# A two-layer hybrid decoder: the rope's exchange of partition blocks moved from a TensorE permutation matmul to on-chip transfers

## The reference, cut to what matters

```
def rope(x, positions):
    ...
    x1, x2 = xf[..., : d // 2], xf[..., d // 2:]
    return jnp.concatenate([x1 * cos - x2 * sin, x2 * cos + x1 * sin], axis=-1).astype(x.dtype)

def swa_branch(q, k, v, positions, sinks):
    ...
    q = rope(q.reshape(B, S, SWA_HEADS, SWA_HEAD_DIM), positions)
    k = rope(k.reshape(B, S, SWA_KV_HEADS, SWA_HEAD_DIM), positions)
```

## Time and profile before

| | |
|---|---|
| median of 3 runs | 1743.79 us (1743.47 to 1743.79) |
| the profiled execution | 1743.34 us |
| its span, first to last instruction | 1741.5 us |
| PE busy | 1713.2 us, 98% of the span |
| PEld, DVE, ACT, POOL busy | 1445.0, 1087.4, 853.1, 142.0 us |
| granted TensorE clock, mean | 0.998 of full |
| DMA engines, HBM read and written | 87 GB/s over the span |

### The profile page before, as it was taken

How to read it: one execution, slowest core, us unless ns; L and a number is a source line. 1 busy time by engine, 2 the same in 40 slices (tenths; PEclk the granted TensorE clock), 3 DMA queues, 4 the chain that set the end, 5 groups by cost and what they waited for, 6 DMA issues and landing times.

```text
span 1741.5 us, 21885 instructions
## 1 busy us (share of the span) xinstructions
PE 1713.2 (98%) x8634; PEld 1445.0 (83%) x8634; DVE 1087.4 (62%) x1494; ACT 853.1 (49%) x1203; POOL 142.0 (8%) x140
## 2 busy tenths in 40 slices
PE   8999999999999999999999999999999999999997
PEld 6888888888898888888888888888888988888886
DVE  7886886675557534354587777867654665343545
ACT  7576566665445414121466755666544453232223
POOL 0111211111200000000001111111111000000000
PEclk9999999999999999999999999999999999999999
DMA  4221122222342222222321211122224222232222
GB/s 155 67 69 61 61 71 64 73 73 85 114 141 73 97 97 97 97 97 97 110 91 64 76 61 61 61 73 73 72 84 156 77 97 97 97 97 97 97 97 73
DMA packets 47638, 152.36 MB, mean 87 GB/s; under 512 B 5296, under 2 KB 9776, under 8 KB 47536
## 3 DMA queue, kind: packets, MB, share of 16 engines
q1 hardware_dynamic: 45520, 147.02, 25.4%
q10 hardware_dynamic: 2016, 3.94, 0.6%
HBM read 146.75 MB, written 4.19 MB: 87 GB/s over the span
## 4 chain that ended last, share of the span: by engine, by line
PE 83%; issue 6%; DVE 5%; ACT 3%; POOL 1%; DMA 1%; SPq 0%; ACTq 0%; DVEq 0%; POOLq 0%
PE bank L557 77%; PE bank L562 3%; PE bank L815 1%; PE bank L866 1%; ACT w_hi L1018 1%; POOL mix L2271 1%; DMA x<-in_x 1%; DVE w_lo L1561 0%; DVE hf L1608 0%; PE bank L566 0%; PE bank L665 0%; DVE x L1617 0%; DVE fb L1807 0%; ACT dn L1075 0%; DVE h_lo L1596 0%
## 5 line engine op out<-in xcount | busy, mean ns | idle before, releaser
L557 PE MATMUL bank<-h_hi,w_hi 128*128 128x512 f32 (+1 forms) x1224 | 477.1, 390 | 7.0 <-DVE h_lo L1596 5.1
L557 PE MATMUL bank<-h_lo,w_hi 128*128 128x512 f32 (+1 forms) x1224 | 471.7, 385 | 0.0
L557 PE MATMUL bank<-h_hi,w_lo 128*128 128x512 f32 (+1 forms) x1224 | 471.6, 385 | 0.0
L1018 ACT ACTIVATE w_hi<-raw 128x1024 fp32r<-128x1024 f32 (+2 forms) x269 | 271.1, 1013 | 219.9 <-DMA raw<-in_w 219.4
L1561 DVE TENSOR_TENSOR w_lo<-raw,w_hi 128x1024 fp32r<-128x1024 f32 (+2 forms) x269 | 316.8, 1181 | 63.9 <-ACT w_hi L1018 57.4
L557 PEld LDWEIGHTS bank<-h_hi,w_hi 128*128 128x128 f32 x1224 | 230.0, 188 | 57.6 <-DVE h_lo L1596 7.3
L557 PEld LDWEIGHTS bank<-h_hi,w_lo 128*128 128x128 f32 x1224 | 229.9, 188 | 46.9
L557 PEld LDWEIGHTS bank<-h_lo,w_hi 128*128 128x128 f32 x1224 | 230.1, 188 | 44.7 <-issue 1.4
L557 PE MATMUL bank<-u_hi,w_hi 128*128 128x512 f32 (+1 forms) x560 | 208.0, 371 | 0.0
L557 PE MATMUL bank<-u_hi,w_lo 128*128 128x512 f32 (+1 forms) x560 | 207.7, 371 | 0.0
L557 PE MATMUL bank<-u_lo,w_hi 128*128 128x512 f32 (+1 forms) x560 | 207.7, 371 | 0.0
(11 more groups left out here) (261 smaller groups left out, 2744.4 us busy)
## 6 DMA issues: line engine op xcount, KB each, us to landing
raw<-in_w SPq DMA_DIRECT2D x251, 512.0 KB, 3.3
x<-in_x SPq DMA_DIRECT2D x16, 256.0 KB, 3.7
side_raw<-in_w SPq DMA_DIRECT2D x6, 512.0 KB, 4.9
x_spill<-x ACTq DMA_DIRECT2D x8, 256.0 KB, 2.2
x<-x_spill SPq DMA_DIRECT2D x8, 256.0 KB, 3.1
out_y<-x SPq DMA_DIRECT2D x8, 256.0 KB, 2.1
raw<-in_w SPq DMA_DIRECT2D x8, 192.0 KB, 2.4
raw<-in_w SPq DMA_DIRECT2D x8, 128.0 KB, 2.3
```

The costliest lines, as they stand in the source:

```text
L557: mm = pe.matmul(o, s, m, start=start and i == 0 and j == 0, stop=last and i == n - 1 and j == 2, skip_group_check=True)
L1018: act.activation(chunk_in(gc, w_hi, side_hi)[:, 0:w], chunk_in(gc, raw, side_raw)[:, 0:w], ACT.Copy)\
```

## The change: what it does

`rp_hi` becomes a float32 copy `rp` of the tile. After it ACT waits until that copy is complete, then (from the second rope tile on) until `rot_used` says that the previous exchanged tile has been read, and then issues four transfers of 32 partitions by 512 floats (64 KB) each, from `rp` to `rp_turned`, each block from its partner. All four count up one semaphore, `rot`, by 16 each. DVE no longer makes `rp_lo`, waits for all four transfers, and reads `rp_turned` in SBUF in place of `rot_bank` in PSUM. `rotate` and its five calls in a layer are gone from TensorE.

```
--- before.py
+++ after.py
@@ -284,8 +284,8 @@
         cf = place("cf", [P, 3, SEQ], F32, r1 + 16384)
         ra = place("ra", [P, SEQ], F32, r1 + 16384 + 6144)
         rb = place("rb", [P, SEQ], F32, r1 + 16384 + 8192)
-        rp_hi = place("rp_hi", [P, SEQ], F32R, r1 + 16384 + 10240)
-        rp_lo = place("rp_lo", [P, SEQ], F32R, r1 + 16384 + 12288)
+        rp = place("rp", [P, SEQ], F32, r1 + 16384 + 10240)
+        rp_turned = place("rp_turned", [P, SEQ], F32, r1 + 16384 + 12288)
         later_f = place("later_f", [P, 768], F32, r1 + 24576)
         later_hi = place("later_hi", [P, 640], F32R, r1 + 24576 + 3072)
         later_lo = place("later_lo", [P, 640], F32R, r1 + 24576 + 5632)
@@ -361,8 +361,7 @@
         mv_ones = signal("mla_v_ones", 2)
         trig_r = signal("trig_scaled", 2)
         rp_h = signal("rope_in_hi", 5)
-        rp_l = signal("rope_in_lo", 5)
-        rot = signal("rotated", 5)
+        rot = signal("rotated", 5 * 4 * 16)
         rot_used = signal("rot_used", 5)
         rp_sum = signal("rope_sum", 5)
         rpo_h = signal("rope_out_hi", 5)
@@ -765,14 +764,6 @@
                     own = slice(h % 2, h % 2 + 2)
                     values(h, CAUSAL, lambda j: (mv_hi[:, j, h // 2, own, :], mv_lo[:, j, h // 2, own, :]))
 
-                def rotate(n):
-                    pe.wait_ge(*rp_l(n + 1))
-                    if n:
-                        pe.wait_ge(*rot_used(n))
-                    pe.matmul(rot_bank[:, :], cst[:, SWAP, :], rp_hi[:, :], start=True, stop=False)
-                    pe.matmul(rot_bank[:, :], cst[:, SWAP, :], rp_lo[:, :], start=False, stop=True)\
-                      .then_inc(rot.sem, 1)
-
                 def band_scores(t):
 
                     pe.wait_ge(*rpo_l(t + 2))
@@ -922,13 +913,10 @@
                             tile(("swa_k",), h_hi, h_lo, None, between)
                         elif h == HEADS - 2:
                             tile(("swa_vt",), h_hi, h_lo, None, between)
-                            rotate(0)
 
                     turn(("swa_v",), ("swa_vt",), vt_at(None))
-                    rotate(1)
                     tile(("swa_q", 1), h_hi, h_lo)
                     band_scores(0)
-                    rotate(2)
                     tile(("swa_q", 2), h_hi, h_lo)
                     pe.wait_ge(*freed(("swa_v",)))
                     pe.wait_ge(*wv_ones(2))
@@ -941,8 +929,6 @@
                         band_shift(n)
                         out_tile(0, n + 1)
                         band_shift(n + 1)
-                        if t < 2:
-                            rotate(t + 3)
                         if t + 1 < PAIRS:
                             tile((("swa_q", 3), ("stick", 0, 0), ("stick", 0, 1))[t], h_hi, h_lo)
                         band_values(n)
@@ -1127,8 +1113,14 @@
                 def rope(n, name, scale):
                     tile_ready(name)
                     if n:
-                        act.wait_ge(*rot(n))
-                    act.activation(rp_hi[:, :], tile_bank(name)[:, :], ACT.Copy, scale=scale).then_inc(rp_h.sem, 1)
+                        act.wait_ge(*rot(4 * 16 * n))
+                    act.activation(rp[:, :], tile_bank(name)[:, :], ACT.Copy, scale=scale).then_inc(rp_h.sem, 1)
+                    act.wait_ge(*rp_h(n + 1))
+                    if n or now[0]:
+                        act.wait_ge(*rot_used(n))
+                    for q in range(4):
+                        to, of_ = (slice(g * HEAD // 2, (g + 1) * HEAD // 2) for g in (q, q ^ 1))
+                        act.dma_start(rp_turned[to, :], rp[of_, :]).then_inc(rot.sem, 16)
 
                 def rope_out(n, dst):
                     act.wait_ge(*rp_sum(n + 1))
@@ -1726,24 +1718,15 @@
                 def rope_in(n, name, scale):
                     dve.wait_ge(*rp_h(n + 1))
                     if n:
-                        dve.wait_ge(*rot(n))
-                    if scale == 1.0:
-                        dve.tensor_tensor(rp_lo[:, :], tile_bank(name)[:, :], rp_hi[:, :].bitcast(F32), ALU.subtract)\
-                           .then_inc(rp_l.sem, 1)
-                    else:
-                        dve.scalar_tensor_tensor(out=rp_lo[:, :], in0=tile_bank(name)[:, :], scalar=scale,
-                                                 in1=rp_hi[:, :].bitcast(F32), op0=ALU.mult, op1=ALU.subtract)\
-                           .then_inc(rp_l.sem, 1)
-                    if n:
                         dve.wait_ge(*rpo_l(n))
                     dve.scalar_tensor_tensor(out=ra[:, :], in0=tile_bank(name)[:, :], scalar=scale, in1=cos_r,
                                              op0=ALU.mult, op1=ALU.mult).then_inc(free_of(name), 1)
 
                 def rope_turn(n, name, dst, hi):
-                    dve.wait_ge(*rot(n + 1))
+                    dve.wait_ge(*rot(4 * 16 * (n + 1)))
                     if n:
                         dve.wait_ge(*rp_sum(n))
-                    dve.tensor_tensor(rb[:, :], rot_bank[:, :], sin_r, ALU.mult).then_inc(rot_used.sem, 1)
+                    dve.tensor_tensor(rb[:, :], rp_turned[:, :], sin_r, ALU.mult).then_inc(rot_used.sem, 1)
                     dve.wait_ge(*rot_used(n + 1))
                     dve.wait_ge(*freed(name))
                     dve.tensor_tensor(ra[:, :], ra[:, :], rb[:, :], ALU.add).then_inc(rp_sum.sem, 1)
```

More of the change, by code:

```diff
@@ L766, in mla_values @@
                     values(h, CAUSAL, lambda j: (mv_hi[:, j, h // 2, own, :], mv_lo[:, j, h // 2, own, :]))
[L768 to L774, removed]
                 def band_scores(t):
@@ L1728, in rope_in @@
                     if n:
[L1729 to L1737, removed]
                         dve.wait_ge(*rpo_l(n))
```

## The result

The changed kernel took 1750.08 us, median of 6 runs (1748.12 to 1751.25); the kernel before, on the same chip, 1743.48 (6 runs, 1742.37 to 1743.79). The ratio is 1.0036 [1.0026, 1.0047]: 6.6 us slower, where 0.5 us faster was forecast, and above the 1747.3 at which the range ended. The profiled execution took 1751.11 us with a span of 1749.2.

A forecast was written before the change was run, and what follows sets the result against it. TensorE was taken to bound nearly everywhere, with PE, ACT and DVE taking turns in the rope's stretch. Per layer -0.46 + 0.44 - 0.2 - 0.50 + 0.59 - 0.1 = -0.23, two layers -0.5: 1743.3 us, range 1739.2 to 1747.3.

The forecast's parts named there:

- I take 0.42 for an issue, with 0.33 and 0.50 as bounds: ACT's price in us per transfer issue, from its eight spills; four after each rope copy, ACT held 1.73 us.
- The 0.05 us for the wait on the copy: Estimated time ACT waits for its own rope copy to end before issuing transfers.
- n = 1: Second rope tile: ACT late for soft_out(7), rotation's saving only lengthens PE's wait; 0.44 us lost per layer.
- n = 4: Fifth rope tile: band_hi(1) late on ACT, 0.59 us lost before PE's wait at band_values(1), per layer.
- n = 2: Third rope tile: transfer lands 0.4 us late for DVE, rp_lo(3) gives 0.60; 0.2 us gained per layer.
- only waits longer: PE at band_scores(0): arrives 0.50 us earlier, chain 0.44 longer, so the removed rotation brings nothing there.
- n = 0: First rope tile: ACT's hold all covered, PE gains the rotation's 0.46 us per layer.
- n = 3: Fourth rope tile: ACT idle until the shift, DVE reads late; PE gains 0.50 us per layer.
- where the prediction counted 0.1: At t = 1, after the fifth rope tile: DVE's tmp stands behind wq_lo, so 0.1 us is gained per layer.
- the whole saving arrives: Rival: issues run beside ACT's compute, all of TensorE's saving arrives, 4.4 us faster, 1739.4 us; chance 0.12.
- The late third tile: Rival: last block lands later than 2.6 us, delaying DVE's third-tile read; past +3.5 us at 4.2 us landing; chance 0.11.
- Four transfers in sequence: Rival: each rope tile's transfers go one behind another, landing 8.9 us after the copy; 1760 us; chance 0.04.

The follow-up runs named there:

- e9_hbm: Kernel before, TensorE still rotating, plus ACT's wait on its copy and four unread transfers per rope tile, 32 partitions by 256 floats, into HBM: 1746.36 us.
- e1_warm: Changed kernel plus eight idle-time matmuls on constants ahead of band_scores(0) and of band_values(1), keeping PE busy in both lengthened waits: 1746.18 us.
- e2_sp: Changed kernel with the same four transfers per rope tile issued by SP instead of ACT: 1740.36 us.
- e7_shared: Kernel with transfers issued by SP, but two of the third rope tile's four issued by ACT: 1739.44 us.
- e8_one: Changed kernel with one 256 KB transfer of the whole tile from ACT instead of four, which exchanges nothing: 1738.90 us.
- e12_n1: Changed kernel with only the second rope tile exchanged by ACT's transfers, the other four turned by TensorE as before: 1749.79 us.
- e10_wide: Kernel before, still rotating, plus ACT's copy wait and four unread transfers per rope tile within SBUF, each 128 partitions by 64 floats: 1753.60 us.
- e5_issues: Kernel before, still rotating, plus ACT's copy wait and four unread half-size transfers per rope tile into a spare SBUF tile: 1753.51 us.
- e4_two: Changed kernel with two 128 KB transfers of 64 partitions from ACT instead of four, not the rope's exchange: 1740.68 us.

## Why the prediction was wrong, step by step

**The step that failed** is "I take 0.42 for an issue, with 0.33 and 0.50 as bounds". Issues of transfers within SBUF take 0.51 us for the first of a group and 0.61 for each that follows. The rows the price was taken from are of transfers to and from HBM, and those to HBM do cost 0.31 and 0.44 in `e9_hbm`. So the nearest rows differed in the one respect that mattered, and the upper bound, the dearest issue of ACT seen, was below the truth. The 0.05 us for the wait on the copy was a guess that no row stood for; wait and gaps together are 0.22 of the 2.57 us, the four issues 2.35. By the sum's own formula a hold of 2.57 us gives, per layer, n = 1 +1.28, n = 4 +1.43, and n = 2 about +0.2; with the other terms as they were that is 1.85 a layer and 1747.5 us, just past the end of the range. The size of this one term turns the sign, then, but doesn't yet give 1750.

**The term that was missing** is PE's clock behind the wait that this makes. The sum has nothing for it, and no rival either: in the prediction PE "only waits longer" at this place. It is 3.9 us of the 6.6, measured by filling the wait.

Place by place, the first layer of `e1_warm` (the chains without the clock) against the kernel before:

- *n = 0, -0.46 predicted.* Right. Rope 1's copy starts at 154.30 instead of 154.80; in `e1_warm` ACT's hold after rope 0 is covered, as argued.
- *n = 1, +0.44.* Right in place and chain, wrong in size: `band_scores(0)` is at 164.56 instead of 163.78, 1.28 later beside PE's 0.50 gain. The links behind ACT (`split`, w_lo, `wq_lo`) kept their lengths to 0.01 us.
- *n = 2, 0.2 gained.* Right, partly by luck: 179.78 - 179.19 is 0.59, 0.19 less than the 0.78 at `band_scores(0)`. DVE reads 3.9 us after the copy, not 3.5, since the last issue starts 1.8 us behind the copy. That costs 0.75 instead of 0.4. But `ra`, which ran beside POOL at 1.05 us before, now misses it and takes 0.69, which gives 0.36 back. `rp_lo(3)` gave its 0.60.
- *n = 3, -0.50, and n = 4, +0.59.* PE is at `band_values(1)` at 192.32 instead of 190.71, so the two together cost 1.61 - 0.59 = 1.02; with 0.50 gained at n = 3, n = 4 lost 1.5. The mechanism is the predicted one, `band_hi(1)` starting 2.57 us behind the copy.
- *Sum.* -0.50 + 1.28 - 0.19 - 0.50 + 1.52 = 1.6 per layer to this point, 3.2 in two; `e1_warm` ended 2.6 us above before, so some 0.3 per layer came back later, where the prediction counted 0.1.

**The rivals.** That the whole saving arrives needed "an issue under about 0.2 us": refuted as it stood. But something near its time, 1739.4 us, comes when ACT's hold is gone: 1740.36 from SP. The late third tile exists (DVE waited 2.4 us in two places in the changed kernel) and was worth 0.9 us (`e2_sp` to `e7_shared`), not the 3.5 it needed; the landing was as taken, and the last of four dear issues started later. Four transfers in sequence: refuted, the median landing of 2.2 us holds with four on the way. The Trainium skill's rule on disjoint partition halves (DMA: Bandwidth & Descriptors, rules for kernel authors) thus can't be read here as one transfer waiting for the other; its advice of one transfer over 128 partitions agrees with `e8_one`, faster than two or four (but without the exchange), though not by its landing, which is the slowest, but by its single issue.

**The chances.** None of the cases held a hold of ACT beyond 4 x 0.50. Even without the clock the time would have been 1746.2, inside the range at its upper end and slower by under 0.2%; the clock made it slower by 0.36%.

**Open.** Why the clock falls behind one wait of 2 us and not behind another is not settled. In the changed kernel's trace three of the four waits of 1.95 to 2.02 us were followed by it, but not the one that ended at 195.30 (1.00 from 194 to 202), and in `e12_n1`'s neither of its two (2.1 and 2.0). In all profiles together, eight of fourteen waits of 1.55 to 2.11 us at these two places were followed by it, and none of those of 1.26 us and less. In `e10_wide` the lower clock had begun before the wait that ended at 193.50 was over (0.59 from 193 to 194). That it follows PE's waits is shown by `e1_warm` alone, where filling two waits kept it at 2.4 GHz. The last 0.3 us per layer were not traced to an instruction.

## What to carry to other kernels

A DMA issue is an instruction in its engine's stream: count every one at its own price, with its group's later ones dearer than the first, and price it from a transfer with the same source and target; where the trace has none, don't let the dearest row of another kind be the upper bound. Before giving a transfer to an engine, see how long that engine waits at this place anyway (1.30 us here: two issues were free, four were not) and who stands behind it; a queue that waits by itself, as SP's does here, takes the same issues without a loss that these runs would show. And when a step makes the bottleneck engine wait 1.6 us or more in dense work, add the possible clock loss as a case of its own, because it can cost more than the wait.

## What the runs showed of the hardware that wasn't expected

- An issue's time depends on whether both ends lie in SBUF, and hardly on bytes or partitions: 0.31 us for the first and 0.44 for the following from SBUF to HBM on ACT; 0.33 from HBM to SBUF on SP; 0.47 to 0.51 and 0.61 within SBUF, at 32 KB and 64 KB alike, over 32 or 128 partitions, on ACT as on SP (0.59).
- Within SBUF, 64 KB landed 2.2 us after the issue in the changed kernel's median (2.0 to 2.6 in the medians of the others), 128 KB 3.0, and 256 KB 3.1, with four on the way in the first case.
- TensorE's granted clock was below 1.00 in up to 8 us of windows (166 to 174) behind a wait of 2.0 us, in some executions and not in others of one kernel: 1746.3 to 1751.8 us for `e12_n1`. It fell as well behind one wait of 1.6 us in `e5_issues`. Behind the lengthened waits of 0.8 and 1.3 us in `e2_sp`, `e4_two` and `e9_hbm` it stayed at 1.00 in the profiled stretch.
